# Attention scores: the causal mask written by ScalarE, minima of negated scores, and the rotary low-part passes of two pieces in the two halves of the array

## The chip, the cores and the metric

The kernel runs on one core of a Trainium2 chip. The metric is the device time of one execution, in microseconds (us); the median of 3 runs before the change is 1550.31 us (1549.93 to 1551.9).

## The reference

One decoder layer over 16 learned meta tokens and 1024 tokens of width 1024. What matters here is its attention part: 8 heads, queries and keys of 128 unrotated and 64 rotated numbers, values of 128 numbers, causal softmax over all earlier positions, in float32.

```
s = einsum('bqhd,bkhd->bhqk', qn, kn) + einsum('bqhd,bkd->bhqk', qr, kr)
s = s.astype(float32) * scale
s = where(kpos <= qpos, s, -inf)
p = softmax(s, axis=-1)
out = einsum('bhqk,bkhd->bqhd', p, vv)
```

Beside it the layer has a state-space part with the same input, and then an output projection and an MLP. The change touches neither of these.

## The kernel before, in words

The program goes through stages: input projections, a latent stage (`phase` before line 1411) that leaves the rotated keys `krT`, attention (`phase_attend`, lines 1411 to 2150), the state-space scan, and the MLP. All five engines get an instruction order that is written out by hand, and semaphores join them. Attention goes head by head (`HEADS` is 8), and within a head block by block (`NT` is 8): block `b` is 128 queries against `width(b)` = 16 + 128(b+1) keys, so 144, 272, 400, 528, 656, 784, 912 and 1040 columns. Two heads make up one turn of a hardware loop; the head's parity is `u`.

Every float32 operand is split into a high part (`hi`, type fp32r) and the rest (`lo`), and a product is the sum of passes hi·hi, hi·lo and lo·hi. For the rotated part 64 rows suffice for a number, so `krT` holds the keys' high part in rows 0 to 63 and their low part in rows 64 to 127, and `qr` holds the queries' high (or low) part twice. One pass with 128 rows gives q_hi·(k_hi + k_lo), another gives q_lo·(k_hi + k_lo).

`scores(h, u, b)` on TensorE (PE, line 1742) writes one block of scores to PSUM. The block lies at column `start(b)` of a flat view of banks 0 to 3 and is cut at bank borders into pieces (`tiles`, lines 1754 to 1755): one piece for b up to 2, two for b from 3 to 6 (264+264, 328+328, 272+512, 512+400), three for b = 7 (250+512+278). For each piece it issues

```
qT hi x kT hi      L1762   start of the sum
mask_b x ident_b   L1765   the last 128 columns of the block alone (bf16)
qT hi x kT lo      L1766
qT lo x kT hi      L1767
qr hi x krT        L1769
qr lo x krT        L1769
```

The mask pass adds a large negative number above the diagonal. PE waits before a block for `a_exp` of block b-2, since two blocks of scores are in PSUM at a time.

What follows on the other engines for block b: VectorE (DVE) reduces the row to its maximum (`most`, line 2001) and multiplies it by -SCALE (line 2003); ScalarE (ACT) takes the exponential with that as bias and adds up the row (`exp`, line 1903); DVE forms the reciprocal and multiplies (`normalise`, lines 2008 and 2010); PE transposes the probabilities (`turn`, line 1786) into two PSUM banks in alternation; ACT copies the high part out (`high`, lines 1895 and 1898) and DVE the low part (`low`, lines 2018 and 2020); then PE multiplies by the values (`weigh`, lines 1797 and 1801), four blocks at a time, and ACT and DVE take the result out (`out`). Between these PE makes the next head's queries and keys in five pieces (`piece`, lines 1717 and 1723; evacuated at 1914 by ACT and 2031 by DVE) and the values of two heads (`values`, line 1739).

The order on PE within a head is: in `late`, for b from 3 to 7, `scores(b)`, then values or a piece where they fall due, at b = 6 `weigh` of the first four blocks, and `turn(b-2)`; then in `next_early` piece 2, scores of the next head's block 0, `turn(6)`, scores of block 1, piece 3, `turn(7)`, scores of block 2, piece 4, `weigh` of the last four blocks, `turn` of the next block 0. `late` and `next_early` on ACT and DVE go in the same order. SyncE and GpSimd (POOL) carry transfers and the state-space preparation.

Of the kernel before, what the change touches and what calls it, by code (L numbers as in the profile page):

```python
# [21 lines left out]
P = 128  # L22
# [84 lines left out]
def setup(nc, io):  # L107
# [17 lines left out]
    k.spare, o = m.at("spare", [P, 640], F32, o)  # L125
# [422 lines left out]
x_in0 x_in1 x_in2 x_in3 x_in4 x_in5 x_in6 x_in7 x_in8 c_in consts id_in mt mt_hi mt_lo mt_turned rs1 sq sqrt ss_set t_hi t_lo turned v zeroed diag rr rr_out  # L548
# [8 lines left out]
a_cut a_e_hi a_e_lo a_exp a_k_in a_mx a_nb a_o_hi a_p a_proj a_q_in a_qr_in a_rs a_s a_t a_t_dup a_t_hi a_t_lo a_v_cut a_v_hi a_v_in a_v_lo a_v_set a_vproj  # L557
# [8 lines left out]
def phase_project(k):  # L566
# [383 lines left out]
    def on_scalar(act):  # L950
# [82 lines left out]
        for n in range(13):  # L1033
# [8 lines left out]
            elif n < 12:  # L1042
                act.activation(k.krT[:, META + c0:META + c0 + 512], src, ACT.Copy).then_inc(sem("lat_hi"), 1)
# [24 lines left out]
    def on_vector(dve):  # L1068
# [166 lines left out]
        for n in range(13):  # L1235
            c0 = 512 * (n % 2)
            src = ps[:, 4 + n % 4, :]
            if n == 12:
# [3 lines left out]
                dve.tensor_copy(mt[:, 2, :], ps[:, 4, 2 * META:3 * META]).then_inc(sem("lat_mt"), 1)  # L1242
# [168 lines left out]
def phase_attend(k):  # L1411
# [25 lines left out]
    assert o <= k.o_wkv  # L1437
    both_at, _ = m.at("s_aT", [P, 2, 2, KD, P], F32R, o_prob - 2 * KD * P * 4)
# [4 lines left out]
    mx, nb, sm, rs, bias = k.st[0], k.st[1], k.st[2], k.st[3], k.st[4]  # L1443
# [5 lines left out]
    STARTS = {3: 3 * 512 - width(3) // 2, 4: 512 - width(4) // 2, 7: 2 * 512 - 250}  # L1449
# [12 lines left out]
    FIRST_BANKS = (7, 6, 1, 2, 5)  # L1462
# [36 lines left out]
    def on_sync(sp):  # L1499
# [113 lines left out]
    def on_gpsimd(pool):  # L1613
# [86 lines left out]
    def on_tensor(pe):  # L1700
# [42 lines left out]
        def scores(h, u, b, first=False):  # L1743
# [12 lines left out]
            d0, d1 = n - P, n  # L1756
            for i, (c0, c1) in enumerate(tiles):
                if b == NT - 1 and i == len(tiles) - 1:
# [3 lines left out]
                pe.matmul(out, qT[u][0][:, q], kT[u][0][:, c0:c1], start=True, stop=False)  # L1762
                lo, hi = max(c0, d0), min(c1, d1)
                if lo < hi:
                    pe.matmul(flat[:, s0 + lo:s0 + hi], k.mask_b[:, :], k.ident_b[:, lo - d0:hi - d0], start=False, stop=False)  # L1765
                pe.matmul(out, qT[u][0][:, q], kT[u][1][:, c0:c1], start=False, stop=False)  # L1766
                pe.matmul(out, qT[u][1][:, q], kT[u][0][:, c0:c1], start=False, stop=False)  # L1767
                for a in range(2):
                    mm = pe.matmul(out, qr[u][a][:, q], k.krT[:, c0:c1], start=False, stop=(a == 1))  # L1769
# [94 lines left out]
        for b in range(3):  # L1864
            scores(0, 0, b, True)
        pe.wait_ge(sem("a_e_lo"), NE)
# [23 lines left out]
    def on_scalar(act):  # L1890
# [9 lines left out]
        def exp(h, b):  # L1900
            n, s0 = width(b), start(b)
            act.wait_ge(sem("a_nb"), NT * h + b + 1)
            act.activation(prob[:, b % 4, 0:n], flat[:, s0:s0 + n], ACT.Exp, bias=nb[:, b:b + 1], scale=SCALE,
                           accum_out=sm[:, b:b + 1]).then_inc(sem("a_exp"), 1)

# [5 lines left out]
        def piece(h, u, n, bank=None):  # L1911
            act.wait_ge(sem("a_proj"), PIECES * h + n + 1)
            for src, dst in evacs(n, u, piece_bank(n) if bank is None else bank):
                act.activation(dst[0], src, ACT.Copy).then_inc(sem("a_e_hi"), 1)
# [8 lines left out]
        def late(h, i, u, more):  # L1923
            for b in range(3, NT):
# [3 lines left out]
                if first:  # L1928
                    exp(h, b)
# [5 lines left out]
                if not first:  # L1935
                    exp(h, b)
# [28 lines left out]
        act.wait_ge(sem("a_v_set"), 2)  # L1965
# [25 lines left out]
    def on_vector(dve):  # L1991
# [5 lines left out]
        def most(h, b):  # L1997
# [3 lines left out]
            dve.tensor_reduce(mx[:, b:b + 1], flat[:, s0:s0 + n], AX.X, ALU.max).then_inc(sem("a_mx"), 1)  # L2001
            dve.wait_ge(sem("a_mx"), NT * h + b + 1)
# [1818 lines left out]
```

## Time and profile before

| | |
|---|---|
| median of 3 runs | 1550.31 us |
| the profiled execution | 1549.37 us, its span 1547.6 us |
| PE busy | 1517.4 us, 98% of the span |
| weight loads (PEld) | 1307.4 us, 84% |
| DVE busy | 1051.6 us, 68% |
| ACT busy | 716.0 us, 46% |
| POOL busy | 781.3 us, 50% |
| chain that ended last | PE 81%, DVE 10%, ACT 2%, DMA 2%, POOL 2%, issue 2% |
| granted TensorE clock | full in all slices (9 of 9 tenths) |

How to read it: times of the trace count from the span's start. A matmul's duration in a row is longer than the distance to the next one, since matmuls are pipelined; so the prediction reads the distance between starts. Attention lies between about 362 and 640 us. An arrow before a name in brackets tells what ended the idle time before a row.

### The profile page before, as it was taken

To read this page: it belongs to the slowest core of one execution; us is meant where nothing else is said; L and a number is where in the kernel's file an instruction comes from. 1 tells how busy PE (TensorE), PEld (TensorE's weight loads), DVE (VectorE), ACT (ScalarE), POOL (GpSimd) and SP (SyncE) were. 2 spreads that over 40 slices of the span, in tenths; PEclk is the share of its full clock that TensorE was granted. 3 is DMA by queue.
4 is the path that set the end of the run, shared out by engine and by line. 5 is a ranking of instruction groups with operands and counts; after the bars stand their busy time and mean duration, and the time that the engine had idled before them with its cause. 6 is when DMAs were issued, how large, how long until landed. Compare 5 with 4: busy or idle time off the path is not lost.

```text
span 1547.6 us, 22730 instructions
## 1 busy us (share of the span) xinstructions
PE 1517.4 (98%) x7919; PEld 1307.4 (84%) x7919; DVE 1051.6 (68%) x1729; ACT 716.0 (46%) x1445; POOL 781.3 (50%) x686
## 2 busy tenths in 40 slices
PE   9999999999999999899999999999999999999997
PEld 8999998878888889788887888788888888888885
DVE  5856516256878778777778789765565677747676
ACT  5232211245656555566664554444444445444542
POOL 7534444134767766953321425776666135405653
PEclk9999999999999999999999999999999999999999
DMA  6444622226556545798878642454444696535666
GB/s 219 113 138 127 181 55 62 68 63 191 167 166 173 163 131 171 236 338 310 313 283 298 238 165 94 149 177 150 150 150 150 218 380 229 192 110 192 195 197 150
DMA packets 225796, 280.64 MB, mean 181 GB/s; under 512 B 21400, under 2 KB 148224, under 8 KB 225696
## 3 DMA queue, kind: packets, MB, share of 16 engines
q1 hardware_dynamic: 224688, 275.69, 54.8%
q0 software_dynamic: 1008, 3.67, 1.3%
q8 instruction: 57, 0.93, 0.2%
q14 instruction: 43, 0.35, 0.1%
HBM read 180.63 MB, written 98.66 MB: 180 GB/s over the span
## 4 chain that ended last, share of the span: by engine, by line
PE 81%; DVE 10%; issue 2%; ACT 2%; DMA 2%; POOL 2%; SPq 0%; DVEq 0%; ACTq 0%; POOLq 0%
PE ps L2981 19%; PE ps L2972 16%; PE ps L825 7%; PE ps L884 6%; PE ps L2842 5%; PE ps L1801 3%; PE ps L2918 3%; PE ps L840 2%; PE ps L856 2%; PE ps L1717 2%; PE ps L1739 2%; PE ps L458 1%; DVE pTlo L2020 1%; PE ps L1769 1%; PE ps L1786 1%
## 5 line engine op out<-in xcount | busy, mean ns | idle before, releaser
L2981 PE MATMUL ps<-dw_hi,df_hi 128*128 128x512 f32 x448 | 174.5, 389 | 1.6 <-DVE dw_lo L3568 1.6
L2981 PE MATMUL ps<-dw_lo,df_hi 128*128 128x512 f32 x448 | 174.3, 389 | 0.0
L2981 PE MATMUL ps<-dw_hi,df_lo 128*128 128x512 f32 x448 | 174.3, 389 | 0.0
L178 POOL TENSOR_TENSOR ring<-stage,zero 128x512 fp32r<-128x512 f32 (+2 forms) x75 | 83.7, 1116 | 150.8 <-DMA stage<-w_in 47.9
L3563 DVE TENSOR_TENSOR df_lo<-df_raw,df_hi 128x512 fp32r<-128x512 f32 x112 | 114.2, 1020 | 49.6 <-ACT df_hi L3259 48.5
L3568 DVE TENSOR_TENSOR dw_lo<-dw_raw,dw_hi 128x512 fp32r<-128x512 f32 x96 | 80.6, 840 | 43.8 <-ACT dw_hi L3268 26.4
L3259 ACT ACTIVATE df_hi<-df_raw 128x512 fp32r<-128x512 f32 x112 | 70.3, 627 | 71.8 <-DMA df_raw<-d_f 71.6
L180 POOL TENSOR_TENSOR ring<-stage,ring 128x512 fp32r<-128x512 f32 (+2 forms) x75 | 100.5, 1340 | 5.9
L2981 PEld LDWEIGHTS ps<-dw_hi,df_hi 128*128 128x128 f32 x448 | 84.1, 188 | 19.5 <-DVE df_lo L3563 2.0
L2981 PEld LDWEIGHTS ps<-dw_lo,df_hi 128*128 128x128 f32 x448 | 84.1, 188 | 17.5
L2981 PEld LDWEIGHTS ps<-dw_hi,df_lo 128*128 128x128 f32 x448 | 84.1, 188 | 17.4
L2842 PE MATMUL ps<-ring,s_aT 128*128 128x512 f32 x384 | 96.8, 397 | 0.5 <-issue 0.4
L825 PE MATMUL ps<-hThi,ring 128*128 128x346 f32 (+1 forms) x480 | 94.4, 325 | 0.0
L3268 ACT ACTIVATE dw_hi<-dw_raw 128x512 fp32r<-128x512 f32 x96 | 60.7, 632 | 70.5 <-POOL dw_raw L2742 24.4
L2842 PEld LDWEIGHTS ps<-ring,s_aT 128*128 128x128 f32 x384 | 70.3, 188 | 15.9 <-issue 1.0
L2918 PE MATMUL ps<-ring,s_aT 128*128 128x512 f32 x336 | 80.7, 397 | 0.9 <-DVE ring L3406 0.5
L884 PE MATMUL ps<-hThi,ring 128*128 128x512 f32 x256 | 80.5, 394 | 0.8 <-DVE dt L1151 0.8
L3253 ACT ACTIVATE fa<-ps 128x512 f32<-128x512 f32 x56 | 33.5, 599 | 100.1 <-DVE ps L3542 81.8
L825 PEld LDWEIGHTS ps<-hThi,ring 128*128 128x128 f32 x480 | 78.7, 189 | 0.2
L2918 PEld LDWEIGHTS ps<-ring,s_aT 128*128 128x128 f32 x336 | 62.3, 188 | 16.2 <-DVE ring L3406 1.1
L2629 POOL TENSOR_TENSOR s_y<-s_y,s_off 128x512 f32<-128x512 f32 x16 | 21.2, 1328 | 89.5 <-DVE s_y L3377 89.5
L1895 ACT ACTIVATE pThi<-ps 128x512 fp32r<-128x512 f32 (+3 forms) x112 | 55.6, 504 | 22.3 <-PE ps L1786 21.2
(543 smaller groups left out, 4536.8 us busy)
## 6 DMA issues: line engine op xcount, KB each, us to landing
df_raw<-d_f SPq DMA_DIRECT2D x112, 256.0 KB, 2.7
d_f<-fa SPq DMA_DIRECT2D x105, 256.0 KB, 2.1
dw_raw<-w_mlp_down SPq DMA_DIRECT2D x96, 256.0 KB, 3.0
landA<-w_mlp_up SPq DMA_DIRECT2D x52, 256.0 KB, 3.2
stage<-w_in SPq DMA_DIRECT2D x40, 256.0 KB, 2.7
stage<-w_out SPq DMA_DIRECT2D x28, 256.0 KB, 5.3
xt<-x SPq DMA_DIRECT2D x8, 512.0 KB, 6.9
d_xT<-xdT SPq DMA_DIRECT2D x8, 512.0 KB, 3.3
```

The lines of the kernel that those rows point to most:

```text
L178: pool.tensor_tensor(hi, src, k.zero[:, 0:1].broadcast_to([P, width]), ALU.add).then_inc(k.sem(fam + "_hi"), 1)
L180: pool.tensor_tensor(lo, src, hi.bitcast(F32), ALU.subtract).then_inc(k.sem(fam + "_cut"), 1)
L825: mm = pe.matmul(ps[:, base + q, 0:w], W[a][:, (8 * c + kk) % RING, P * j:P * j + P], hT[b][:, kk, c0:c0 + w], start=(kk == 0 and (a, b) = ...
L884: mm = pe.matmul(ps[:, g % 4, :], W[a][:, (8 * c + kk) % RING, P * j:P * j + P], hT[b][:, kk, c0:c0 + 512], start=(kk == 0 and (a, b) == ( ...
L2842: mm = pe.matmul(ps[:, MIX, :], aT[a][:, (t + 1) % 2, kk, :], W[b][:, KD * c + kk, :], start=(nth == 0 and (a, b) == (0, 0)), stop=(nth == ...
L2918: mm = pe.matmul(ps[:, unit_banks(i)[g], :], s[a][:, kk, :], W[b][:, KD * c + kk, :], start=(kk == 4 * g and (a, b) == (0, 0)), stop=(kk = ...
L2972: mm = pe.matmul(bank, mats[i % 2][q][a][:, kk, :], MOVING[q][b][:, kk, :], start=(fresh and kk == 0 and (a, b) == (0, 0)), stop=(last and ...
L2981: mm = pe.matmul(ps[:, base + t, :], F_AT[q % SLOTS][a][:, P * t:P * t + P], W_AT[q % SLOTS][b][:, :], start=(fresh and (a, b) == (0, 0)), ...
L3259: act.activation(F_AT[s][0][:, :], F_RAW[s][:, :], ACT.Copy).then_inc(sem("d_fhi"), 1)
L3268: act.activation(W_AT[s][0][:, :], src, ACT.Copy).then_inc(sem("d_whi"), 1)
L3563: dve.tensor_tensor(F_AT[s][1][:, :], F_RAW[s][:, :], F_AT[s][0][:, :].bitcast(F32), ALU.subtract).then_inc(sem("d_flo"), 1)
L3568: dve.tensor_tensor(W_AT[s][1][:, :], src, W_AT[s][0][:, :].bitcast(F32), ALU.subtract).then_inc(sem("d_wlo"), 1)
```

## The change

Four things are done in `phase_attend` and in the two places that fill `krT`:

- Keys are scaled. The evacuations of `kT` and `krT` multiply by -SCALE, on ACT and on DVE, so that scores come out negated and scaled. DVE then takes the row's minimum, which is the exponential's bias as it stands; the multiplication of line 2003 and its wait go away.
- The mask pass on PE (L1765) goes away. ACT instead writes zeros and the masking number to the last piece of block b+2 right after it has taken the exponential of block b (`fill`), after a wait for its own exponential; PE waits for `a_fill` before that piece and adds to what lies there. The mask row is built once by POOL. The last-but-one piece of a block is issued first, the masked one second.
- The q_lo pass of the two lowest pieces of a block that has several is made 64 rows deep: q_lo·k_hi alone. One piece uses rows 0 to 63 of the array with `krT`; the other uses rows 64 to 127 with `krT_low`, a copy of the high part of the first 512 keys in those rows, made by one DMA at the start. These two come last in the block. The product q_lo·k_lo is left out for them.
- Block 5 starts elsewhere, so that its pieces are 392+392, and block 7 has 256+512+272. The first pass of block 7's lowest piece is written twice, over the whole bank (512 columns). Banks 1 and 2 change places in the first head, and ACT writes the first two fills before it takes out the first head's pieces.

```
     STARTS = {3: ..., 4: ..., 5: 3 * 512 - width(5) // 2, 7: 2 * 512 - 256}
-    FIRST_BANKS = (7, 6, 1, 2, 5)
+    FIRST_BANKS = (7, 6, 2, 1, 5)
...
+        sp.dma_start(krT_low[ROPE:P, :].bitcast(F32), k.krT[0:ROPE, 0:512].bitcast(F32)).then_inc(sem("a_kr_low"), 16)
...
     def scores(h, u, b, first=False):
+            if len(tiles) > 1:
+                tiles[:2] = tiles[1::-1]
+            halves = sorted(tiles)[1::-1] if len(tiles) > 1 else []
+            for c0, c1 in tiles:
+                if masked:
+                    pe.wait_ge(sem("a_fill"), NT * h + b + 1)
+                if whole:
+                    pe.matmul(ps[:, 1, :]..., qT[u][0][:, q], kT[u][0][:, 0:c1].unsqueeze(1).broadcast_to([P, 2, c1]), start=True, ...)
+                else:
+                    pe.matmul(out, qT[u][0][:, q], kT[u][0][:, c0:c1], start=not masked, ...)
-                if lo < hi:
-                    pe.matmul(flat[:, s0 + lo:s0 + hi], k.mask_b[:, :], k.ident_b[:, lo - d0:hi - d0], ...)
                 pe.matmul(out, qT[u][0][:, q], kT[u][1][:, c0:c1], ...)
                 pe.matmul(out, qT[u][1][:, q], kT[u][0][:, c0:c1], ...)
                 for a in range(2):
+                    if a == 0 or (c0, c1) not in halves:
                         mm = pe.matmul(out, qr[u][a][:, q], k.krT[:, c0:c1], ...)
+            for (c0, c1), rope, rows in zip(halves, (k.krT, krT_low), (slice(0, ROPE), slice(ROPE, P))):
+                mm = pe.matmul(flat[:, s0 + c0:s0 + c1], qr[u][1][rows, q], rope[rows, c0:c1], start=False, stop=True, ...)
...
     def exp(h, b, more=True):
-            act.activation(prob..., ALU Exp, bias=nb[:, b:b + 1], scale=SCALE, ...)
+            act.activation(prob..., ALU Exp, bias=least[:, b:b + 1], scale=-1.0, ...)
+            if b + 2 < NT or more:
+                act.wait_ge(sem("a_exp"), NT * h + b + 1)
+                fill((b + 2) % NT)
+    def fill(b):
+            c1 = start(b) + width(b)
+            c0 = max(start(b), (c1 - 1) // 512 * 512)
+            act.activation(flat[:, c0:c1], k.mask_row[:, 400 - (c1 - c0):400], ACT.Copy).then_inc(sem("a_fill"), 1)
...
-    dve.tensor_reduce(mx[:, b:b + 1], flat[:, s0:s0 + n], AX.X, ALU.max).then_inc(sem("a_mx"), 1)
-    dve.wait_ge(sem("a_mx"), NT * h + b + 1)
-    dve.tensor_scalar(nb[:, b:b + 1], mx[:, b:b + 1], -SCALE, None, ALU.mult).then_inc(sem("a_nb"), 1)
+    dve.tensor_reduce(least[:, b:b + 1], flat[:, s0:s0 + n], AX.X, ALU.min).then_inc(sem("a_nb"), 1)
...
-    dve.tensor_tensor(dst[1], src, dst[0].bitcast(F32), ALU.subtract)
+    dve.scalar_tensor_tensor(dst[1], src, -SCALE, dst[0].bitcast(F32), ALU.mult, ALU.subtract)   # keys alone
```

How it stands in the order of PE, at block 3 of an even head (`kT0hi` is the high part of the keys of an even head, `qr0lo` the low part of its rotated queries). Before:

```order
L1762 MATMUL ps<-kT0hi,qT0hi 128x264
L1765 MATMUL ps<-ident_b,mask_b 128x128
L1766 MATMUL ps<-kT0lo,qT0hi 128x264
L1767 MATMUL ps<-kT0hi,qT0lo 128x264
L1769 MATMUL ps<-krT,qr0hi 128x264
L1769 MATMUL ps<-krT,qr0lo 128x264
L1762 MATMUL ps<-kT0hi,qT0hi 128x264
L1766 MATMUL ps<-kT0lo,qT0hi 128x264
L1767 MATMUL ps<-kT0hi,qT0lo 128x264
L1769 MATMUL ps<-krT,qr0hi 128x264
L1769 MATMUL ps<-krT,qr0lo 128x264
```

and now (`krT_low` lies in memory of `pTlo`, so its row is named that):

```order
L1779 MATMUL ps<-kT0hi,qT0hi 128x264
L1780 MATMUL ps<-kT0lo,qT0hi 128x264
L1781 MATMUL ps<-kT0hi,qT0lo 128x264
L1784 MATMUL ps<-krT,qr0hi 128x264
L1774 REGISTER_ALU
L1779 MATMUL ps<-kT0hi,qT0hi 128x264
L1780 MATMUL ps<-kT0lo,qT0hi 128x264
L1781 MATMUL ps<-kT0hi,qT0lo 128x264
L1784 MATMUL ps<-krT,qr0hi 128x264
L1786 MATMUL ps<-krT,qr0lo 128x264
L1786 MATMUL ps<-pTlo,qr0lo 128x264
```

The mask pass is gone, the two q_lo passes stand side by side at the end, and there is a wait (the register row) before the second, masked piece.

On ACT, from the end of a head's last exponential to the transposes of block 6 (`prob<-ps,stat_52` is an exponential, `pThi` a high part of transposed probabilities, `kT1hi` a piece of the next head's keys). Before:

```order
L1903 ACTIVATE prob,stat_53<-ps,stat_52 128x1040
L1912 REGISTER_ALU
L1914 ACTIVATE kT1hi<-ps 128x346
L1902 ISA
L1903 ACTIVATE prob,stat_53<-ps,stat_52 128x144
L1893 REGISTER_ALU
L1895 ACTIVATE pThi<-ps 128x4x128
```

and now:

```order
L1921 ACTIVATE prob,stat_53<-ps,stat_52 128x1040
L1930 ACTIVATE ps<-mask_row 128x272
L1938 REGISTER_ALU
L1940 ACTIVATE kT1hi<-ps 128x346
L1920 ISA
L1921 ACTIVATE prob,stat_53<-ps,stat_52 128x144
L1930 ACTIVATE ps<-mask_row 128x400
L1911 REGISTER_ALU
L1913 ACTIVATE pThi<-ps 128x4x128
```

Two fills (of the next head's blocks 1 and 2) now stand ahead of the copies of block 6's transposes.

## Rows read from the trace of the kernel before

**Rows 1.** Busy us by stretch: start:end, length, PE, PEld, DVE, ACT, POOL, clock, DMA.

```profile
489.40:502.20 12.80, 12.42 (x85) 11.07 (x83) 11.55 (x28) 9.13 (x23) 11.17 (x17) 1.00 0.48 154
502.20:518.00 15.80, 15.73 (x109) 14.62 (x110) 10.32 (x26) 7.46 (x18) 10.95 (x16) 1.00 0.72 200
```

**Rows 2.** Waits from 362.5 to 633: engine, line, released by, us, times, longest.

```profile
PEld ps L1786 <- DVE pTlo L2020: 4.1, 8, 0.8
PEld ps L1797 <- DVE pTlo L2020: 3.4, 8, 0.6
```

**Rows 3.** Timeline of PE at block 6 of an odd head: start us, us, instruction.

```profile
483.40 0.71 PE L1786 MATMUL ps<-ident,prob 128*128 128x128 f32 x5
...
484.14 0.23 PE L1765 MATMUL ps<-ident_b,mask_b 128*128 128x128 bf16 x1
484.18 0.43 PE L1766 MATMUL ps<-kT1lo,qT1hi 128*128 128x400 f32 x1
484.45 0.34 PE L1767 MATMUL ps<-kT1hi,qT1lo 128*128 128x400 f32 x1
484.63 0.34 PE L1769 MATMUL ps<-krT,qr1hi 128*128 128x400 f32 x1
```

**Rows 4.** Timeline of PE, last head: three 16-row matmuls (L1820) between 128-row ones.

```profile
631.81 0.28 PE L1769 MATMUL ps<-krT,qr1hi 128*128 128x250 f32 x1
631.92 0.28 PE L1769 MATMUL ps<-krT,qr1lo 128*128 128x250 f32 x1
632.13 0.49 PE L1820 MATMUL ps<-xdt_hi,s_bthi 16*128 16x512 f32 x1
632.47 0.39 PE L1820 MATMUL ps<-xdt_lo,s_bthi 16*128 16x512 f32 x1
632.70 0.39 PE L1820 MATMUL ps<-xdt_hi,s_btlo 16*128 16x512 f32 x1
633.02 0.77 PE L1786 MATMUL ps<-ident,prob 128*128 128x128 f32 x5
```

**Rows 5.** Timeline of the weight loads in the same place.

```profile
632.13 0.18 PEld L1820 LDWEIGHTS ps<-xdt_hi,s_bthi 16*128 16x128 f32 x1
632.24 0.18 PEld L1820 LDWEIGHTS ps<-xdt_lo,s_bthi 16*128 16x128 f32 x1
```

**Rows 6.** Timeline of PE near the start: 128-row matmuls behind a 16-row one.

```profile
38.13 0.25 PE L491 MATMUL ps<-diaglo,ones 16*128 16x16 f32 x1
38.31 0.50 PE L494 MATMUL ps<-diaghi,ones 128*128 128x512 f32 x1
38.65 0.40 PE L494 MATMUL ps<-diaglo,ones 128*128 128x512 f32 x1
```

**Rows 7.** Timeline of DVE between block 7's reduction and block 5's low parts.

```profile
492.90 1.23 DVE L2001 TENSOR_REDUCE stat<-ps 128x1 f32<-128x1040 f32 x1
494.16 0.15 DVE L2003 TENSOR_SCALAR stat<-stat 128x1 f32<-128x1 f32 x1
494.34 0.28 DVE L2018 TENSOR_TENSOR pThi<-ps,pThi 16x128 fp32r<-16x128 f32 x1
```

**Rows 8.** Timeline of PE: the waits before `turn(6)` and before the second `weigh`.

```profile
494.63 0.28 PE L1769 MATMUL ps<-krT,qr0lo 128*128 128x144 f32 x1
495.25 1.12 PE L1786 MATMUL ps<-ident,prob 128*128 128x128 f32 x8 [0.34 <-DVE pTlo L2020]
...
501.85 0.32 PE L1723 MATMUL ps<-ckThi,wklo 128*128 128x346 f32 x1
502.27 0.50 PE L1797 MATMUL ps<-pThi,v 128*128 128x512 f32 x1
```

**Rows 9.** Groups of ACT by shape: busy us, mean ns, idle before.

```profile
L3069 ACT ACTIVATE ps<-mask_b 128x512 f32<-128x512 bf16 x30 | 18.4, 612 | 0.0
L1895 ACT ACTIVATE pThi<-ps 128x256 fp32r<-128x256 f32 x16 | 6.1, 381 | 0.2
```

**Rows 10.** Timeline of PE: block 2 of the first head.

```profile
364.92 0.42 PE L1762 MATMUL ps<-kT0hi,qT0hi 128*128 128x400 f32 x1 [0.71 <-ACT prob L1903]
```

More of the change, by code:

```diff
@@ L1042, in on_scalar @@
             elif n < 12:
-                act.activation(k.krT[:, META + c0:META + c0 + 512], src, ACT.Copy).then_inc(sem("lat_hi"), 1)
+                act.activation(k.krT[:, META + c0:META + c0 + 512], src, ACT.Copy, scale=-SCALE).then_inc(sem("lat_hi"), 1)
             else:
@@ L1437, in phase_attend @@
     assert o <= k.o_wkv
+    krT_low = pT[1][:, 0, :]
     both_at, _ = m.at("s_aT", [P, 2, 2, KD, P], F32R, o_prob - 2 * KD * P * 4)
@@ L1755, in scores @@
             tiles = [(c - s0, d - s0) for c, d in zip(cuts[:-1], cuts[1:])][::-1]
-            d0, d1 = n - P, n
-            for i, (c0, c1) in enumerate(tiles):
-                if b == NT - 1 and i == len(tiles) - 1:
+            if len(tiles) > 1:
+                tiles[:2] = tiles[1::-1]
+            halves = sorted(tiles)[1::-1] if len(tiles) > 1 else []
+            for c0, c1 in tiles:
+                if b == NT - 1 and c0 == 0:
                     pe.wait_ge(sem("a_exp"), NT * h + b)
@@ L1761, in scores @@
                 q = slice(P * b, P * b + P)
[L1762 to L1767 removed]
+                masked, whole = c1 == n, b == NT - 1 and c0 == 0
+                skip = masked or whole
+                if masked:
+                    pe.wait_ge(sem("a_fill"), NT * h + b + 1)
+                if whole:
+                    pe.matmul(ps[:, 1, :].rearrange("p (a b) -> p a b", a=2), qT[u][0][:, q],
+                              kT[u][0][:, 0:c1].unsqueeze(1).broadcast_to([P, 2, c1]), start=True, stop=False, skip_group_check=skip)
+                else:
+                    pe.matmul(out, qT[u][0][:, q], kT[u][0][:, c0:c1], start=not masked, stop=False, skip_group_check=skip)
+                pe.matmul(out, qT[u][0][:, q], kT[u][1][:, c0:c1], start=False, stop=False, skip_group_check=skip)
+                pe.matmul(out, qT[u][1][:, q], kT[u][0][:, c0:c1], start=False, stop=False, skip_group_check=skip)
                 for a in range(2):
[L1769 removed]
+                    if a == 0 or (c0, c1) not in halves:
+                        mm = pe.matmul(out, qr[u][a][:, q], k.krT[:, c0:c1], start=False, stop=(a == 1), skip_group_check=skip)
+            for (c0, c1), rope, rows in zip(halves, (k.krT, krT_low), (slice(0, ROPE), slice(ROPE, P))):
+                mm = pe.matmul(flat[:, s0 + c0:s0 + c1], qr[u][1][rows, q], rope[rows, c0:c1], start=False, stop=True, skip_group_check=c1 == n or b == NT - 1 and c0 == 0)
             mm.then_inc(sem("a_s"), 1)
@@ L1913, in piece @@
             for src, dst in evacs(n, u, piece_bank(n) if bank is None else bank):
-                act.activation(dst[0], src, ACT.Copy).then_inc(sem("a_e_hi"), 1)
+                act.activation(dst[0], src, ACT.Copy, scale=-SCALE if PIECE[n][0] == "k" else 1.0).then_inc(sem("a_e_hi"), 1)
         def values(i, n):
@@ L1928, in late @@
                 if first:
-                    exp(h, b)
+                    exp(h, b, more)
                     if more:
@@ L1935, in late @@
                 if not first:
-                    exp(h, b)
+                    exp(h, b, more)
                 for n in V_AT.get(b, ())[1:] if u == 0 else ():
@@ L1963, in next_early @@
             high(h + 1, 0)
-        act.wait_ge(sem("a_v_set"), 2)
+        act.wait_ge(sem("a_v_set"), 5)
+        act.wait_ge(sem("qro_step0"), 2 * NT)
+        for b in range(2):
+            fill(b)
         for n in range(PIECES):
@@ L2064, in late @@
                     normalise(h, b - 1)
-                most(h, b)
+                smallest(h, b)
                 if b == NT - 1 and not more:
@@ L2084, in next_early @@
         def next_early(h, u, last=False):
-            most(h + 1, 0)
+            smallest(h + 1, 0)
             normalise(h, NT - 1)
@@ L2088, in next_early @@
             low(h, NT - 2)
-            most(h + 1, 1)
+            smallest(h + 1, 1)
             piece(h + 1, 1 - u, 3)
             low(h, NT - 1)
-            most(h + 1, 2)
+            smallest(h + 1, 2)
             normalise(h + 1, 0)
@@ L2104, in on_vector @@
         for b in range(3):
-            most(0, b)
+            smallest(0, b)
             if b:
```

31 lines of the change are left out of this document (20 added, 11 removed).

## The prediction

> **What bounds the kernel now.** I read the busy shares first: PE is at work 98% of the span, so time goes down only where PE gets less to do or where it stands waiting. Then I cut attention into stretches. In the 15.80 us from a head's second `weigh` on (502.2), through the next head's blocks 3 to 5, PE is busy 15.73 us, DVE 10.32: PE alone sets the pace there. From the end of the `weigh` at block 6 (489.4) to the next `weigh` (502.2) PE is busy 12.42 of 12.80 us, but DVE 11.55 and ACT 9.13 [rows 1]. In that stretch PE stops twice in each head. In the list of waits its weight loads wait 8 times for DVE's low parts before `turn` (4.1 us) and 8 times before `weigh` (3.4 us) [rows 2]. On the timeline these are the step of 0.62 us behind a 144-column pass, and that of 0.42 us behind a 346-column one [rows 8]. So a head has two parts: blocks 3 to 6, ruled by PE, and from `weigh` to `weigh`, ruled by DVE and ACT, in which PE saved is mostly wait gained. I measure PE by the distance between starts: 0.23 us for 512 columns, 0.11 for 250 [rows 4], 0.18 for 400 [rows 3], hence, along that line, 0.12 for 264, 0.15 for 328 and 0.18 for 392.
>
> **The mask pass, removed.** It starts at 484.14 and the next pass at 484.18, so it costs 0.04 itself; but that next pass then takes 0.27 us where 0.18 is usual [rows 3]. Together 0.13 us a block. Blocks 3 to 6 of 8 heads are 32 blocks: **-4.2 us** on the path. The other 32 (blocks 7, 0, 1, 2) lie in the stretch that DVE rules.
>
> **The two half-deep passes.** They save the shorter of the two pieces if they run side by side: 0.12 (264), 0.15 (328), 0.18 (392), 0.18 (400) in blocks 3 to 6, that is 0.63 us a head and 5.0 us in all; 0.11 in block 7. But they are the first passes here that don't take all 128 rows, and the array has to go into that form and back in every block. The trace has no 64-row matmul; the nearest rows are three 16-row ones among 128-row ones. Going in, the 250-column pass before them takes 0.21 us up to the next start instead of 0.11, and the first 16-row one 0.34 instead of 0.23 [rows 4]: its weights begin to load at 632.13, with the matmul and not under the one before it [rows 5]. So 0.10 + 0.11. Going out to transposes, the last takes 0.32 instead of 0.23, and five transposes 0.77 instead of 0.71 [rows 3, 4]: 0.09 + 0.06. Going out to full matmuls, the first of 512 columns takes 0.34 again [rows 6]; with the same 0.09 ahead of it, 0.20. A visit thus costs 0.41 us where a piece or values follow and 0.36 where transposes follow. By the order of PE, of the 32 visits in blocks 3 to 6 values, pieces or `weigh` follow 24 and transposes follow 8 (blocks 3 and 4 of odd heads): 24 x 0.41 + 8 x 0.36 = 12.7 us. Less the 5.0 saved, **+7.7 us**. I take the 16-row price because the cause that the rows show (weights that can't be loaded under the matmul before) has nothing to do with the number of rows. Below, the bound is a visit that costs nothing (-5.0); above, that the second half also waits for its own load, 0.11 behind the first [rows 5], in pieces that are about equal (+3.5), or that the halves run one after the other (+5.0).
>
> On the visits the skill has two rules. The Trainium skill's TensorEngine Tiling page (Tiling Modes, Key Properties) says that a change of the tiling mode drains the engine, while tiles of one mode load and multiply in parallel. By that the 64-row form pays at both ends as the 16-row one does, and the second half doesn't wait; the sum stays as it is. No run here has yet shown a 64-row tile.
>
> **From `weigh` to `weigh`.** PE loses four mask passes (-0.5 a head). It gets block 7's visit (0.36 - 0.11) and a first pass of 512 columns for one of 250 (+0.12), so that it would arrive about 0.15 us earlier and wait longer. What counts is DVE and ACT. DVE is rid of the multiplication behind each minimum: the next instruction starts 0.18 us behind its start [rows 7], and it stands before `low(5)`, whose end releases `turn(6)`. ACT gets a fill for each block. The kernel already writes a mask to PSUM in another stage, 0.61 us for 512 columns; with the slope from there to a copy of 256 columns at 0.38 [rows 9], about 0.9 ns a column, fills take 0.28 (144 columns) to 0.51 (400). The fills of the next head's blocks 1 and 2, 0.40 + 0.51, now stand ahead of the copies of block 6's transposes, for which DVE's `low(6)` and PE's `turn(7)` wait. ACT has 12.80 - 9.13 = 3.67 us free in the stretch [rows 1], most of it while it waits for PE. I let the two cancel: **0**. Bounds: both multiplications on the chain saved and nothing lost, -0.36 a head, -2.9 in all; half of the two fills shows, +0.45 a head, +3.6 in all.
>
> **The rest.** In blocks 3 to 6 the fills cost nothing: ACT's own idle time covers them (it is busy 7.46 of 15.80 us there [rows 1]), and block b's fill is queued two blocks ahead of its use. Without that cover each would show with its 0.4 to 0.5 us in PE's wait for `a_fill`. The multiplication by -SCALE in the evacuations changes the form of an instruction, not their number; nothing, under the same cover. The DMA of 128 KB to `krT_low` is due only at block 3 of the first head; the transfers queued behind it on SyncE are for the next head, whole heads away. POOL's few extra operations come once, before ACT's first fill. At the start of attention ACT now writes two fills (0.28 + 0.40) ahead of the first head's pieces, and one (0.51) between the exponential of block 0 and the scores of block 2, where PE already waits 0.71 us for ACT [rows 10]; some of the first overlaps with PE's matmuls: **+0.8 us**, between 0.3 and 1.2.
>
> **Sum.** -4.2 + 7.7 + 0 + 0.8 = +4.3 us on the profiled execution's 1549.4, which lies 0.9 under the median of the runs; on the median of 1550.3 that makes **1554.6 us**. With the smaller uncertainties (the stretch, the start) its own range is 1552 to 1558. A measurement of this kernel can tell about 0.2%, 3.1 us, from no change.
>
> **Rivals.**
> *The half passes come free (faster).* If weights of a 64-row half load under the passes before and the array doesn't pause, then the visits cost nothing and 5.0 us are saved: -4.2 - 5.0 + 0.8 = -8.4, **1541.9 us**. It decides from a price of a visit under 0.16 us, where it equals the mean saving (5.0/32). For it: both halves lie in different rows and different PSUM banks, and in [rows 3, 4] weights otherwise always load ahead. Against it: [rows 4, 6], at all three borders. The Trainium skill's TensorE page (Part 3, The mechanism) speaks for this rival: a weight load for another row group is pulled ahead of matmuls in flight, and packed matmuls start some 4 ns apart. The trace has not borne it out for rows 0 to 15 among full passes [rows 5].
> *Half price (no change).* The pause is paid on both sides (0.10 + 0.09) and the loads are hidden: 32 x 0.19 = 6.1, less 5.0, less 4.2, plus 0.8: -2.3, **1548.0 us**. For it: a half leaves the other rows' weights alone. Against it: the loads in [rows 5].
> *Dearer.* The second half waits for its load, or runs behind the first (+3.5 to +5.0), or ACT's fills hold up `low(6)` and `turn(7)` (+3.6): about **1558.5 us**. For it: ACT's order at the end of a head, and that loads stand 0.11 apart [rows 5]. Against it: ACT's free 3.67 us.
>
> **How the numbers follow.** The forecast has 0.50, free passes 0.22, half price 0.13, dearer 0.15. Of the forecast's half, 0.36 lies above 1553.4 (+0.2%) and 0.14 below. Half price gives 0.08 to no change and 0.05 to faster. So faster 0.22 + 0.05 = 0.27; no change 0.14 + 0.08 = 0.22; slower 0.36 + 0.15 = 0.51. The range from 1542.0 to 1559.5 leaves out half of the free case (0.11) and 0.06 of the dearer one. Cases of both signs hold most of the chance; the likeliest one's own range is the 1552 to 1558 above.
>
> **What would show it.** Right: the first half pass of a block starts 0.1 us late, the pass behind the pair too, and the pass after that is long by 0.11; the row of mask passes is gone and no full pass before takes 0.09 too long in its place; waits before `turn` and `weigh` add up to about what they are. Wrong: the two half passes start within a few ns of each other and the next pass one piece later without a gap (free); PE waits for `a_fill`, or the waits for `pTlo` grow by more than 0.3 us a head (dearer).

## The result and the profile after

The changed kernel takes **1555.17 us** (median of 7 runs, 1553.97 to 1557.49), the kernel before 1550.31 beside it: a ratio of 1.0032, with an interval of 1.0021 to 1.0043. It is slower by 0.3%, and the forecast was 1554.6. Medians and ratios leave out executions that took over 1.5% longer than the fastest of their kernel, at a lower granted clock. The profiled execution of the changed kernel took 1557.49 us, the longest of the seven and 2.3 above their median, with a span of 1555.6. The page's busy times:

```profile
PE 1524.1 (98%) x7855; PEld 1303.2 (84%) x7855; DVE 1047.3 (67%) x1665; ACT 742.0 (48%) x1509; POOL 779.4 (50%) x689
```

PE issues 64 matmuls fewer, the mask passes, and yet is busy 6.7 us longer; ACT has 26 us more (the fills), DVE 4 us less. The stretches that answer to [rows 1], of the changed kernel, in the same columns:

```profile
493.83:506.76 12.93, 12.56 (x81) 10.81 (x79) 11.52 (x25) 10.27 (x25) 10.80 (x17) 1.00 0.43 139
506.76:522.56 15.80, 15.80 (x108) 14.37 (x108) 9.25 (x23) 8.27 (x21) 11.31 (x17) 1.00 0.72 205
```

In blocks 3 to 5 PE sets the pace as before. The waits of the changed kernel in attention (engine, line, released by, us, times, longest), of which the first two answer to [rows 2]:

```profile
PEld ps L1803 <- DVE pTlo L2047: 3.5, 11, 0.5
PEld ps L1814 <- DVE pTlo L2047: 1.8, 7, 0.3
...
PE ps L1779 <- ACT ps L1930: 2.1, 4, 1.2
PE ps L1803 <- DMA pTlo<-krT: 1.0, 1, 1.0
PE ps L1837 <- POOL xdt_lo L1693: 1.0, 1, 1.0
```

The waits for DVE's low parts fell from 7.5 to 5.3 us. Three others stand beside them. The waits for the copy and for POOL, and the longest of the four for ACT's fills, lie at attention's two ends; the other three for fills (0.26, 0.26 and 0.38 us) lie where heads meet.

**Where the time went.** I set the start of every `weigh` in one trace against the same in the other; a head has a stretch from its first to its second `weigh` (blocks 7, 0, 1, 2) and one from there to the next head's first (blocks 3 to 6). Differences to the kernel before in us, one profiled execution each ("fills later" is without pairs):

```
                           after  pair   no     fills  two     copy
                                  alone  pair   later  visits  early
first scores               +0.57  +0.28  +0.53  +0.33  +1.16   +1.14
to the first weigh         +3.24  +2.66  -0.23  -0.35  +3.88   +0.53
blocks 3-6, odd (mean)     +0.25  +0.83  -0.24  -0.29  +2.41   +0.32
blocks 3-6, even (mean)    +0.44  +0.93  -0.06  -0.31  +2.57   +0.45
weigh to weigh (sum of 7)  +0.07  -0.05  -1.34  -1.72  +3.75   +0.11
last head, to its weigh    +1.63  +0.14  +0.24  +0.05  +1.43   +0.48
```

The first column belongs to the change (means over three heads), the others to experiments below. In the change the three odd and three even stretches make +2.1, the ends +5.4, and 0.4 lies behind the last head's first `weigh`: 8.0 us between the spans. 2.3 of these are this execution's distance from its own median and 0.9 that of the execution before.

**The pair.** PE at block 3 of an even head, and the loads of the two halves, in the changed kernel (start us, us, instruction):

```profile
512.80 0.29 PE L1781 MATMUL ps<-kT0hi,qT0lo 128*128 128x264 f32 x1
512.92 0.28 PE L1784 MATMUL ps<-krT,qr0hi 128*128 128x264 f32 x1
513.13 0.39 PE L1786 MATMUL ps<-krT,qr0lo 64*128 64x264 f32 x1
513.14 0.38 PE L1786 MATMUL ps<-pTlo,qr0lo 64*128 64x264 f32 x1
513.45 0.38 PE L1746 MATMUL ps<-wvhi,ckThi 128*128 128x256 f32 x1
513.67 0.28 PE L1746 MATMUL ps<-wvlo,ckThi 128*128 128x256 f32 x1
513.79 0.28 PE L1746 MATMUL ps<-wvhi,ckTlo 128*128 128x256 f32 x1
```
```profile
513.13 0.18 PEld L1786 LDWEIGHTS ps<-krT,qr0lo 64*128 64x128 f32 x1
513.13 0.18 PEld L1786 LDWEIGHTS ps<-pTlo,qr0lo 64*128 64x128 f32 x1
```

The two halves start 0.01 us apart and their weights load together: they do run side by side. But the pass before takes 0.21 up to the next start where 0.12 is usual, the pair 0.32 where its 264 columns would take 0.12 (its loads start with the matmuls, not ahead of them), and the first pass behind 0.22 instead of 0.12. That is 0.09 + 0.20 + 0.10 = 0.39 us, for the 0.12 of the piece saved.

**The mask.** The full passes now follow each other in even steps, as here at block 5 of an odd head; the step of 0.27 us of [rows 3] is gone:

```profile
484.20 0.34 PE L1784 MATMUL ps<-krT,qr1hi 128*128 128x392 f32 x1
484.38 0.34 PE L1779 MATMUL ps<-kT1hi,qT1hi 128*128 128x392 f32 x1
484.56 0.34 PE L1780 MATMUL ps<-kT1lo,qT1hi 128*128 128x392 f32 x1
484.74 0.34 PE L1781 MATMUL ps<-kT1hi,qT1lo 128*128 128x392 f32 x1
```

Adding up starts to starts in an even head's blocks 3 to 6 (502.27 to 525.38 before, 506.83 to 530.43 after): the mask passes together with the passes of `kT` lo, which come behind them, 1.81 before, 1.33 after (-0.48); the passes of `qr` 2.64 and 3.14 (+0.50); values 6.65 and 6.91, pieces 3.01 and 3.21, which pay for the way out (+0.46). Together +0.48.

**The ends.** PE at the first head, and PE at block 6 of the last head:

```profile
364.28 0.28 PE L1784 MATMUL ps<-krT,qr0lo 128*128 128x272 f32 x1
365.73 0.42 PE L1779 MATMUL ps<-kT0hi,qT0hi 128*128 128x400 f32 x1 [1.17 <-ACT ps L1930]
...
366.54 0.35 PE L1784 MATMUL ps<-krT,qr0lo 128*128 128x400 f32 x1
367.93 0.44 PE L1803 MATMUL ps<-ident,prob 128*128 128x128 f32 x2 [1.04 <-DMA pTlo<-krT]
...
368.40 0.42 PE L1780 MATMUL ps<-kT0lo,qT0hi 128*128 128x264 f32 x1
368.62 0.42 PE L1781 MATMUL ps<-kT0hi,qT0lo 128*128 128x264 f32 x1
...
629.22 0.49 PE L1837 MATMUL ps<-xdt_hi,s_bthi 16*128 16x512 f32 x1 [0.95 <-POOL xdt_lo L1693]
```

PE waits 1.17 us for ACT's fill of block 2 (0.71 before, [rows 10]), then 1.04 for the copy to `krT_low` (it lies in memory of `pTlo`). After that a pass of 264 columns takes 0.22 us instead of 0.12. The stretches (columns as in [rows 1]; the last but two is the granted clock):

```profile
364.50:368.10 3.60, 1.39 (x8) 1.02 (x7) 1.95 (x7) 2.44 (x8) 0.00 (x0) 1.00 0.42 117
368.10:371.50 3.40, 3.40 (x16) 2.93 (x16) 1.35 (x4) 1.17 (x5) 0.00 (x0) 0.53 0.75 216
...
631.20:634.60 3.40, 3.40 (x10) 2.29 (x9) 2.59 (x8) 2.07 (x6) 3.17 (x4) 0.51 0.00 0
...
648.00:652.00 4.00, 3.54 (x10) 2.28 (x10) 3.66 (x6) 3.11 (x8) 3.92 (x3) 0.57 1.04 402
```

Where PE stood still for 2.2 us of 3.6, the granted clock fell to about half in the next 3.4 us, the lower of the two levels (1.2 GHz of 2.4); PE got half as much done there, some 1.6 us lost. The same came at 631.2, behind the wait of 0.95, and a third time near 648, in the last head. In the profile of the kernel before the clock is full in these places.

### The profile page after: what moved, and what is told of

The parts are those of the page before. It is cut to its first block, busy times and chain, and to the rows that moved or that the text cites. A ratio compares the mean times of both kernels' runs of the same rounds, so it can differ in the third digit from the quotient of the medians.

```text
span 1555.6 us, 22628 instructions
## 1 busy us (share of the span) xinstructions
PE 1524.1 (98%) x7855; PEld 1303.2 (84%) x7855; DVE 1047.3 (67%) x1665; ACT 742.0 (48%) x1509; POOL 779.4 (50%) x689
## 4 chain that ended last, share of the span: by engine, by line
PE 84%; DVE 7%; ACT 4%; DMA 2%; POOL 2%; issue 2%; SPq 0%; DVEq 0%; ACTq 0%; POOLq 0%
PE ps L3011 19%; PE ps L3002 16%; PE ps L826 7%; PE ps L885 6%; PE ps L2872 5%; PE ps L1818 3%; PE ps L2948 3%; PE ps L841 2%; PE ps L857 2%; PE ps L1803 2%; PE ps L1746 2%; PE ps L459 1%; PE ps L2826 1%; PE ps L1784 1%; ACT pThi L1913 1%
## 5 line engine op out<-in xcount | busy, mean ns | idle before, releaser
L3593 DVE TENSOR_TENSOR df_lo<-df_raw,df_hi 128x512 fp32r<-128x512 f32 x112 | 119.6, 1068 | 50.8 <-ACT df_hi L3289 50.4
```

The costliest lines, as they stand in the source:

```text
L3593: dve.tensor_tensor(F_AT[s][1][:, :], F_RAW[s][:, :], F_AT[s][0][:, :].bitcast(F32), ALU.subtract).then_inc(sem("d_flo"), 1)
```

## Experiments

Each was timed in turn with the kernel before on the same chip. First the parts by themselves.

**The pair taken out of the changed kernel** (with its copy and the wait for it):

```diff
-            halves = sorted(tiles)[1::-1] if len(tiles) > 1 else []
+            halves = []
-        sp.dma_start(krT_low[ROPE:P, :].bitcast(F32), ...).then_inc(sem("a_kr_low"), 16)
-        pe.wait_ge(sem("a_kr_low"), 16)
```

> The change without its half-deep passes: all low passes have 128 rows, and the copy of the rotated keys with its wait is gone; mask by ScalarE and minima stay. Theory (a visit to the 64-row form costs 0.41 or 0.36 us, a pair saves 0.15): the time falls by about 7.7 us for the 32 visits of blocks 3 to 6 less nothing for block 7, and by some 2.7 us more, the 1.0 us wait for the copy in the first head and the 1.7 us that the half-clock stretch behind it costs; 1555.2 - 9 = about 1546, that is 4 us faster than before the change. Rival (the pair is free or a gain, the loss is the fills on ScalarE and the start): about 1555 to 1560. In the trace, a head's part from its second weigh to its first one should be shorter by 0.8 to 0.95 us than in the change.

1548.37 us (11 runs), ratio 0.9987 [0.9978, 0.9997]. So the pairs, the copy and its wait cost 6.8 us (1555.17 less 1548.37), and the sign of the change is theirs. It is not as fast as expected, 2.4 us short, and a head's blocks 3 to 6 are 0.49 (odd) and 0.50 (even) shorter than in the change, where 0.80 to 0.95 was expected. The table shows why not: in even heads these blocks gain 0.06 on the kernel before, where the mask passes alone should give 0.52.

**The pair alone, put into the kernel before** (its mask passes, maxima and bank order kept):

```diff
+            halves = sorted(tiles)[1::-1] if len(tiles) > 1 else []
...
                 for a in range(2):
+                    if a == 0 or (c0, c1) not in halves:
                         mm = pe.matmul(out, qr[u][a][:, q], k.krT[:, c0:c1], ...)
+            for (c0, c1), rope, rows in zip(halves, (k.krT, krT_low), (slice(0, ROPE), slice(ROPE, P))):
+                mm = pe.matmul(flat[:, s0 + c0:s0 + c1], qr[u][1][rows, q], rope[rows, c0:c1], start=False, stop=True)
```

> The kernel before with the half-deep passes alone: the mask pass on the tensor engine and maxima stay. Theory: 1550.3 + 7.7 for the visits of blocks 3 to 6, + 0 to 2 for block 7 (its stretch is ruled by VectorE), + 1 to 2.7 for the wait for the copy of the keys and a half-clock stretch behind it: 1559 to 1562. Rival (the pair itself gains 5 us): about 1545 to 1548. In the trace the two passes of a pair start within 0.01 us of each other, 0.1 us late, and the first full pass behind them is long by 0.1.

1558.59 us (4 runs), ratio 1.0054 [1.0038, 1.0070], 8.4 us by the ratio and 8.9 by the medians of that chip. In blocks 3 to 6 the table has +0.83 (odd) and +0.93 (even). The prediction's prices make 0.97 and 1.07 of it: block 5 keeps its pieces of 272 and 512 columns here, so a head's pairs save 0.57, not 0.63. A visit thus cost 0.35 and 0.38 on average. Against this kernel the changed one is 0.58 and 0.49 a head shorter: the mask passes, forecast at 0.52, and some 0.06 for block 5's new cut. Most of the rest is the start: PE waits for the copy here too, behind a wait of 0.72 for ACT, but the clock behind the two stays full:

```profile
368.05 0.44 PE L1792 MATMUL ps<-ident,prob 128*128 128x128 f32 x2 [1.57 <-DMA pTlo<-krT]
...
368.05:371.45 3.40, 3.40 (x26) 3.08 (x27) 1.97 (x6) 0.69 (x2) 0.00 (x0) 1.00 0.68 190
```

**Each half in a visit of its own**, right behind the four full passes of its piece:

```diff
+                if (c0, c1) in halves:
+                    rope, rows = ((k.krT, slice(0, ROPE)), (krT_low, slice(ROPE, P)))[halves.index((c0, c1))]
+                    mm = pe.matmul(out, qr[u][1][rows, q], rope[rows, c0:c1], start=False, stop=True, ...)
-            for (c0, c1), rope, rows in zip(halves, ...):
-                mm = pe.matmul(...)
```

> The change with the two half-deep passes of a block apart: each stands behind the full passes of its own piece, so that the array goes into the 64-row form twice per block and nothing runs side by side. Theory (price per visit): each of the 32 blocks 3 to 6 gets one more visit into full passes, 0.40 us, and the saved shorter piece back, 0.16: +0.56 x 32 = +18 us; block 7 adds 0 to 4: 1573 to 1577. Rival (the price is not for going in and out, but once per pair or for the first pass of a block): only the 5 to 6 us of the lost overlap, about 1561.

1575.7 us (4 runs), ratio 1.0160 [1.0144, 1.0176]: +20.5 us on the change. A second way in and out costs 2.15 us a head more in blocks 3 to 6 (2.41 - 0.25, 2.57 - 0.44), 0.54 for each of 4 blocks, where another visit at the forecast's 0.41 and a piece that no longer runs beside the other, 0.15, would give 0.56. PE in this kernel:

```profile
487.22 0.28 PE L1784 MATMUL ps<-krT,qr1hi 128*128 128x264 f32 x1
487.43 0.38 PE L1787 MATMUL ps<-pTlo,qr1lo 64*128 64x264 f32 x1
487.74 0.39 PE L1779 MATMUL ps<-kT1hi,qT1hi 128*128 128x264 f32 x1
487.97 0.29 PE L1780 MATMUL ps<-kT1lo,qT1hi 128*128 128x264 f32 x1
```

0.21, 0.31 and 0.23: a single half of 264 columns takes as long as the pair. So the second half of a pair is free, and the price is the way in and out.

**What the mask and the minima give.** The kernel without pairs, and without any mask: no fills, no wait for them, one first pass in block 7 instead of two. The causal mask within a block's last 128 columns is left out.

```diff
-            if b + 2 < NT or more:
-                act.wait_ge(sem("a_exp"), NT * h + b + 1)
-                fill((b + 2) % NT)
...
-                if masked:
-                    pe.wait_ge(sem("a_fill"), NT * h + b + 1)
...
-    start=not masked
+    start=True
```

> No half-deep passes, minima, and no mask at all: neither ScalarE's fills nor a mask pass, nor the double first pass of block 7 (each query also sees the later keys of its last 128). Theory after the run without half-deep passes (there the fills stand ahead of the copies of the values on ScalarE, and the tensor engine waits for these in even heads): the 0.52 us per head that the mask passes cost in blocks 3 to 6 now shows in full, and the start is 0.8 us shorter: 1548.4 - 4 to 5 = about 1543.5 to 1544.5. Rival (the fills cost nothing, as the prediction had it for blocks 3 to 6; something else eats the mask's gain): 1547.5 to 1548.5.

1545.92 us (10 runs, 1542.39 to 1550.64), ratio 0.9970 [0.9957, 0.9983], between the theory and its rival. From `weigh` to `weigh` it is 3.17 us shorter than the kernel before (sum of seven); without pairs but with the fills it was 1.34, or 1.72 with the fills later. And **the minima alone**: that kernel with the mask pass of PE put back (it also has the change's cuts and its order of pieces).

```diff
+                if masked:
+                    pe.matmul(flat[:, s0 + n - P:s0 + n], k.ident_b[:, :], k.mask_row[:, 400 - P:400], start=False, stop=False)
```

> The kernel before with negated keys and minima alone: the mask pass is back on the tensor engine (the identity as weights, the mask row as the moving operand), no fills, no half-deep passes; pieces are cut and ordered as in the change. Theory (VectorE rules the stretch from weigh to weigh and loses a multiplication twice on its chain, 0.18 us each): up to 2.9 us less than before, 1547.5 to 1549.5. Rival (the multiplication was hidden): 1550.

1548.17 us (11 runs), ratio 0.9986 [0.9977, 0.9995]: -2.2 us. In its profile -1.2 of them lie in seven stretches from `weigh` to `weigh`, and the means of blocks 3 to 6 are within 0.1 of nothing. That fits a multiplication behind each reduction that stood on the path in the part that DVE rules, and there alone; the cuts and the order of pieces, which came along, were not timed by themselves.

**The fills at a later place in ACT's order**, without pairs: behind the copies of values, pieces and transposes, and in the last head behind the state-space preparation.

```diff
-            if b + 2 < NT or more:
-                act.wait_ge(sem("a_exp"), NT * h + b + 1)
-                fill((b + 2) % NT)
+        def fill_after(h, b, more=True):
+            if b + 2 < NT or more:
+                act.wait_ge(sem("a_exp"), NT * h + b + 1)
+                fill((b + 2) % NT)
...
                 if not more:
                     scan_start(b)
+                fill_after(h, b, more)
```

> No half-deep passes; mask by ScalarE and minima as in the change, but each fill stands later in ScalarE's order: behind the copies of values, pieces, outputs and transposes that the tensor engine waits for, and in the first head behind pieces 1 and 2. Theory (the fills' cost is their place): nearly as without any mask, 1544 to 1546, that is faster than both kernels by 4 to 6 us over the one before. Rival (the fills cost nothing): 1548.4 as without the half-deep passes.

1546.92 us (11 runs), ratio 0.9980 [0.9971, 0.9989]: it beats the kernel before and the changed one, but is 0.9 us short of the expected 1544 to 1546. ACT and PE with the fill in its first place (no pairs), between the exponential of block 5 and the next head's first piece:

```profile
516.48 0.51 ACT L1928 ACTIVATE ps<-mask_row 128x400 f32<-128x400 bf16 x1
516.92 0.58 ACT L1945 ACTIVATE v<-ps 128x512 fp32r<-128x512 f32 x1
```
```profile
518.13 0.28 PE L1745 MATMUL ps<-wvhi,ckTlo 128*128 128x256 f32 x1
518.47 0.49 PE L1723 MATMUL ps<-cqThi,wqhi 128*128 128x512 f32 x1
518.80 0.40 PE L1723 MATMUL ps<-cqTlo,wqhi 128*128 128x512 f32 x1
```

and with the fill later:

```profile
515.53 0.59 ACT L1947 ACTIVATE v<-ps 128x512 fp32r<-128x512 f32 x1
516.01 0.51 ACT L1930 ACTIVATE ps<-mask_row 128x400 f32<-128x400 bf16 x1
```
```profile
517.32 0.28 PE L1745 MATMUL ps<-wvhi,ckTlo 128*128 128x256 f32 x1
517.43 0.39 PE L1723 MATMUL ps<-cqThi,wqhi 128*128 128x512 f32 x1
517.66 0.39 PE L1723 MATMUL ps<-cqTlo,wqhi 128*128 128x512 f32 x1
```

The step to the piece is 0.34 with the fill ahead of the copy of the values and 0.11 with the fill behind it, and the step behind that 0.33 and 0.23: together 0.33, about all that this head's blocks 3 to 6 gain. Even heads' blocks 3 to 6 go from -0.06 to -0.31. They stop short of -0.52: in the even head's sum of steps the mask's two rows lose 0.49, and 0.10 comes back in the `qr` passes, behind which PE waits for `turn` (0.15 to 0.39 in two odd heads). That some 0.3 is left without any mask too (-0.22 and -0.32 in the kernel without one) fits: what the mask gives up there goes to DVE.

**The same order of fills with the pairs kept:**

> The change with all half-deep passes, and the fills later in ScalarE's order as in the run beside it. Theory (a visit costs its 0.41 or 0.36 us whatever ScalarE does): slower than the run beside it by 7.7 us for blocks 3 to 6 and 1 to 2.7 us for the copy of the keys: about 1553.5 to 1555. Rival (the pairs cost because they delay ScalarE and VectorE, not the tensor engine): within 3 us of the run beside it.

1554.19 us (7 runs), ratio 1.0028 [1.0017, 1.0039]: the fills' place is worth little under the pairs (blocks 3 to 6: +0.26 and +0.37), and pairs cost 7.3 us here. In its profile PE waits 1.35 us for the fill of block 2 and 1.17 for the copy; the half clock behind them lasts twice as long as in the change, and the stretch to the first `weigh` is +4.65:

```profile
367.10:370.50 3.40, 2.70 (x12) 2.43 (x12) 1.15 (x5) 1.82 (x5) 0.00 (x0) 0.50 0.68 187
370.50:373.90 3.40, 3.40 (x17) 3.20 (x16) 1.80 (x3) 0.24 (x1) 2.22 (x3) 0.50 0.83 227
```

**The ends.** Matmuls that nobody reads, in the three long waits of PE, to see whether its pauses bring the half clock:

```diff
+            if b == 2:
+                idle_work(TURN, 5)
             scores(0, 0, b, True)
+        idle_work(TURN, 5)
         pe.wait_ge(sem("a_kr_low"), 16)
...
+                    for _ in range(4):
+                        pe.matmul(ps[:, PROJ, :], qT[1][0][:, 0:P], k.krT[:, 0:512], start=True, stop=True)
                 pe.wait_ge(sem("p_xwlo"), g + 1)
```

> The change with matmuls that nobody reads in three waits of the tensor engine: five before the scores of the first head's block 2, five before its wait for the copied keys, four before the state-space matmuls of the last head. Theory (behind these waits the granted clock falls to half for about 3.4 us, in which half the work is lost): the half-clock stretches near 368 and 631 us disappear, each worth 1.7 us, and the waits stay as they are: 1555.2 - 2 to 3.4 = about 1552 to 1553. Rival (the slow stretches have nothing to do with the waits before them): no change, 1555, and the slow stretches are still there.

1555.6 us (6 runs), ratio 1.0032 [1.0019, 1.0044]: no gain, against the expectation. In its profile the two stretches are at full clock, and the one near 648 of the change is still there (start:end as before):

```profile
368.10:371.50 3.40, 3.40 (x28) 3.12 (x28) 1.78 (x5) 1.43 (x4) 0.00 (x0) 1.00 0.72 202
...
631.00:634.60 3.60, 3.54 (x23) 2.79 (x22) 3.27 (x7) 2.32 (x6) 3.44 (x4) 1.00 0.00 0
...
641.40:644.80 3.40, 1.63 (x15) 1.32 (x13) 3.01 (x5) 2.50 (x6) 3.32 (x4) 1.00 0.63 211
644.80:648.20 3.40, 3.07 (x11) 2.11 (x12) 2.64 (x5) 2.83 (x6) 3.24 (x4) 0.62 0.93 336
```

This profiled execution (1554.32 us) is 3.2 us shorter than that of the change, which was the longest of its seven, but the ratios are equal (1.0032): the profile fits the expectation, and the times don't bear it out. The stretch near 648 needs neither the pairs nor the fills: profiles without pairs have one that begins at 636 to 639, and so has that of the minima alone, which has no fills either.

**The copy issued earlier** on SyncE, ahead of its wait for the rotated queries, and the same with **ACT's state-space preparation ahead of the fill** in the last head:

```diff
+        sp.dma_start(krT_low[ROPE:P, :].bitcast(F32), ...).then_inc(sem("a_kr_low"), 16)
         for q in range(2):
             sp.wait_ge(sem(f"qr_sent{q}"), 32 * NT // 2)
-        sp.dma_start(krT_low[ROPE:P, :].bitcast(F32), ...).then_inc(sem("a_kr_low"), 16)
```

> The changed kernel, with the copy to krT_low issued by SyncE ahead of its wait for the rotated queries' transfers instead of behind it. In the changed kernel the copy is issued at 365.63 and PE waits 1.04 us for it before turn(0,0); behind the last transfer before (issued at 361.85) it would be issued near 362.6 and land near 365. Theory (the copy's wait is a term of its own, and the half-clock stretch behind it comes from PE's pauses): the wait is gone and the stretch at half clock near 368 too, so 1.0 + 1.7 less, about 1552.5 us. Rival (the wait is gone, but a stretch at half clock comes sooner or later all the same): 1.0 less, about 1554.2 us. Second rival (something else is late there, the probabilities of block 0): no change, 1555.2 us.

> As the run with the early copy, and ScalarE does the state-space preparation of the last head (xdt_hi) ahead of the fill instead of behind exponential and fill. The fill takes 0.5 us, so PE's wait of 0.95 us for POOL at 629 falls to about 0.45. Theory (pauses of PE bring on the half clock): the stretch near 631 may go too, 0.5 to 2.2 less than the run with the early copy, about 1550.5 to 1552. Rival (half clock comes all the same): 0.5 less, about 1553.7 us.

1554.33 us (9 runs), ratio 1.0027 [1.0017, 1.0037], and 1553.67 (11 runs), 1.0020 [1.0011, 1.0029]: 0.8 and 1.9 us under the change by ratio, with intervals that overlap its own. PE in the first of them, at the start and in the last head:

```profile
367.10 0.34 PE L1784 MATMUL ps<-krT,qr0lo 128*128 128x400 f32 x1
367.28 0.38 PE L1803 MATMUL ps<-ident,prob 128*128 128x128 f32 x2
...
627.34 0.50 PE L1837 MATMUL ps<-xdt_hi,s_bthi 16*128 16x512 f32 x1 [0.96 <-POOL xdt_lo L1693]
```
```profile
365.10:368.70 3.60, 2.43 (x18) 2.25 (x17) 1.92 (x7) 2.48 (x8) 0.00 (x0) 1.00 0.47 124
368.70:372.10 3.40, 3.40 (x29) 3.27 (x30) 2.43 (x7) 2.59 (x8) 0.00 (x0) 1.00 0.72 209
```

The wait for the copy is gone, the clock behind it is full, and the first head's stretch is +0.53 (+1.00 in the second kernel) instead of +3.24. With the preparation first, the last head's is +0.03 instead of +1.63, though PE then waits 0.53 us for the fill instead. The times moved by less than these profiles, to where the rivals had them (1554.2 and 1553.7). That fits stretches at half clock that don't come in every run, which is not shown; both profiles, like that of the change, have one more, at 644 (648 there).

## Why the prediction was right, and where it was not

**The pair, right.** +7.7 was forecast for the visits of blocks 3 to 6. The pair alone confirms it there: 0.83 and 0.93 a head, each measured over three heads, make 7.0 for eight, though the last head shows only 0.14. The price of 0.41 and 0.36, taken from 16-row matmuls [rows 4 to 6], fits 64-row ones within 0.04. The times of whole kernels lie around 7.7 as well (pair alone 8.4 to 8.9, taken out 6.8, taken out with the fills later 7.3), but that is partly luck, since they hold more than this term: PE's wait of 1.0 to 1.6 us for the copy and what the clock does behind it, and in the last two block 7's pair with 1.4 to 1.7, while blocks 3 to 6 give back only 0.5 to 0.7 a head there. The Trainium skill's TensorEngine Tiling page (Tiling Modes, Key Properties) has both halves of it: a change of mode drains the engine (0.21 instead of 0.12 ahead of the pair), tiles of one mode run in parallel (0.01 us apart). The rival of free passes had the second half right and failed on the first: both loads start with their matmuls at 513.13, not under the full pass before. The Trainium skill's TensorE page (Part 3, The mechanism), which the prediction read in this rival's favour, lets a load be pulled ahead when its row group doesn't conflict with the matmuls in flight; the passes ahead of a pair fill all 128 rows, so that rule doesn't promise it. "Half price" failed on the same row, "dearer" on the two loads that start together and on the waits for `pTlo`, which fell.

**The mask, right in size.** -4.2 was forecast. The even head's starts give -0.48, which makes -3.8 for eight heads; the -0.53 between the pair alone and the change has block 5's new cut in it. A fill takes 0.30 to 0.51 us, as estimated. But "in blocks 3 to 6 the fills cost nothing: ACT's own idle time covers them" holds only because the pairs make PE late. Without them the fill ahead of the copy of the values shows with 0.33 us at one piece of an even head, and with the fills later or gone PE waits for DVE instead.

**From `weigh` to `weigh`: right number, wrong reason.** 0 was forecast since DVE's gain and ACT's fills were let cancel, and +0.07 over seven was measured. But four terms meet there, read from single profiles. The minima give 1.2 (minima alone). The mask passes taken off PE, with no fills in their place, give 2.0 more (3.17 less 1.2), where the prediction took PE's saving for wait gained. ACT's fills, with the doubled first pass of block 7, take back 1.8 of that (3.17 less 1.34), or 1.5 at their later place: they do cost, and PE waits for them at three of the seven places. The last 1.4 (+0.07 against -1.34) goes to block 7's pair, which the prediction counted at nothing because it would only lengthen a wait. In the kernel before it does (pair alone, -0.05); with DVE faster it doesn't.

**The start, wrong.** "The DMA of 128 KB to `krT_low` is due only at block 3 of the first head" was false: PE's wait for it stands ahead of `turn(0)`, SyncE issued it at 365.63 behind its wait for the rotated queries, and PE stood 1.04 us. The +0.8 was meant for the fills alone, and with the copy early the ends of its stretch give 1.2 (first scores +1.14, then +0.53, of which 0.44 is blocks 3 to 6 of an even head), though the first scores come 0.15 to 0.52 us later in kernels without early fills too, so how much of that the fills cost is not shown. The half clock behind the two pauses was not foreseen.

**The last head, not in the sum at all.** ACT's fill (0.50 us) stands ahead of the preparation of the state-space part, and POOL and then PE wait for that one: 0.95 us of PE, none before, in one profile with the half clock behind it. The order of ACT shows it in the diff's `exp`; I had followed the fills only where heads meet.

**The sum.** It came out within 0.6 us because two errors met, which is luck. The steady part was forecast at 3.5 (0.39 a head odd, 0.49 even) and measured at 2.8 (0.25 and 0.44, four times each). The ends were forecast at 0.8 and are 4.8 in this profile (0.57, 3.24 less 0.44, 1.63 less 0.25); but this execution lies 2.3 above its median, and that of the kernel before 0.9 below; if both distances lie at the ends, which no run shows, they cost some 1.6 in a usual one. What is left, 0.5, lies from `weigh` to `weigh` and behind.

## What to carry to other kernels

Price a change of the array's form by its borders: going in and out cost about 0.4 us here, with 16 rows as with 64, so a pair of half-deep passes pays only where what it saves between two borders is more than that, or, by the same prices, where several share one visit, which no run here tried. A cost "hidden by idle time" is hidden by the engine that is late, so when two edits come together, take one out and look again: in blocks 3 to 6 the fills were nearly free only under the pairs. And of every added wait, look at where it stands in the waiting engine's order and at what the issuing queue waits for, not at where its data are used.

## What was unexpected in the hardware

Pauses of PE of 1.17 and 1.04 us within 3.6 us were followed by 3.4 us at half the clock (0.53), pauses of 1.35 and 1.17 in the same place by 6.8 us (pairs with the fills later, 0.50), and one of 0.95 by 3.4 (0.51). Yet pauses of 0.72 and 1.57 (pair alone), and one of 0.96 (early copy), were followed by a full clock. What decides it stays open. With the waits filled, the stretches behind them were at full clock and the one near 648 stayed, and the medians show no gain.
